# Fused transformer blocks, the first projection: x and the first weight unit lead the transfers, and x is turned between the unit's chunks

## Chip, cores and metric

The kernel runs on one core of one Trainium2 chip. The metric is the device time in microseconds (us) of one execution; lower is better.

## What is computed

Two stacked transformer blocks on x (256 tokens, 2048 channels, float32). The change touches only the first step of the first layer: a norm, and the product with the weights of queries, keys and values.

```python
def rms_norm(x, gain):
    xf = x.astype(jnp.float32)
    y = xf * lax.rsqrt(jnp.mean(xf * xf, axis=-1, keepdims=True) + EPS) * gain.astype(jnp.float32)
    return y.astype(x.dtype)

def first_block(x, ...):
    h = x
    for i in range(DEPTH):
        hn = rms_norm(h, mix_norm[i])
        # i == 0: mixer_a begins with qkv = h @ w_qkv, (256, 2048) x (2048, 3072)
        h = h + mixer_a(hn, ...)   # i == 1: mixer_b
        h = h + conv_ffn(rms_norm(h, ffn_norm[i]), ...)
    return rms_norm(h, final_norm)
# after it two layers of a second block (four attention kinds each), on the result
```

## The kernel before

All weights stream through in units of 1 MB (128 partitions x 2048 values). SyncE loads a unit into one of five `raw` buffers (`load_unit`, L216), ScalarE makes its rounded high part (`split_high`, L234) and VectorE the low rest, in place of `raw` (`split_low`, L242). TensorE multiplies each 128-row chunk with three products, high by high, low by high and high by low (`three`, L259 to L261), so that the result is near float32. Work on a unit is ordered by counting semaphores: `w_high`, `w_low`, and `w_used`, which TensorE raises after a unit. Since `high` has three buffers, the split of unit u waits until unit u-3 is used.

`qkv_product` (L773) is the first stage: 24 units, 6 column groups of 512 columns with 4 units each. Each unit holds 4 of the 16 row chunks; for each of the two 128-token tiles a unit takes 4 chunks x 3 matmuls, so 24 matmuls of 128x512 in all. The left operand, x transposed and multiplied by the norm's gain, in a high and a low part (`hh`, `hl`), is made once at the start, in four groups g of 512 channels. `Boundary` holds its steps:

- `turn(pe, g)` (L425 to L440): 8 transposes (L438) of the group into two banks, given by `SUM_BANK` = (4, 6, 0, 2).
- `high(act, g)` (L447): four ScalarE copies of 256 columns (L451) from the banks into `hh`, times the gain.
- `low(dve, g)` (L457): four VectorE steps (L462) into `hl`; the last raises `h_low`.
- `square(act, g)` (L480): sums of squares for the norm, which is applied only to the results.

The gains come from four tables (`mix_norm`, `ffn_norm`, `pre_norm_g_2`, `final_norm`), loaded as 112 rows, transposed once on TensorE (L918), copied by VectorE into `gain` (L882, semaphore `g_taken`).

The order is written out by hand for each engine. SyncE issues `ident` and the four tables (L816 to L820), then x group 0, unit 0, x group 1, unit 1, x groups 2 and 3, units 2 to 4. TensorE waits for the tables, transposes them, then turns x groups 0 to 3, one behind the other, and only then takes unit 0. ScalarE does `high(0)`, the split of unit 0, `high(1)`, the split of unit 1, `high(2)`, `high(3)`, then the split of unit 2; VectorE follows in the same order with the low parts. Everything behind this stage (attention, output product, feed-forward, the other layers) is not touched.

Of the kernel before, what the change touches and what calls it, by code (L numbers as in the profile page):

```python
# [21 lines left out]
F32 = mybir.dt.float32  # L22
F32R = mybir.dt.float32r
ALU = mybir.AluOpType
# [313 lines left out]


SUM_BANK = (4, 6, 0, 2)  # L340


class Boundary:
# [19 lines left out]
        return (0 if self.kind == "load" else 8, 16 if self.kind == "final" else 8, 2 if self.kind == "final" else 1)  # L363

    def bank(self, g, t):
        return self.c.bank[SUM_BANK[g] + t]

    def cols(self, t, g):
        return self.c.x[:, t, g * 512:(g + 1) * 512]
# [73 lines left out]

        return sum(b.kind in ("post", "end") for b in self.c.boundaries[0:self.n])

    def high(self, act, g):
        c = self.c  # L447
        act.wait_ge(c.x_turned, 4 * self.n + g + 1)
        for k in range(4):
            kt = 4 * g + k  # L450
            ins = act.activation(c.hh[:, kt, :], self.bank(g, k // 2)[:, k % 2 * S:(k % 2 + 1) * S], ACT.Copy,  # L451
                                 scale=c.gain[:, self.gain_col + kt:self.gain_col + kt + 1])
            if k % 2:
                ins.then_inc(c.h_high, 1)

    def low(self, dve, g):
        c = self.c  # L457
        for k in range(4):
            kt = 4 * g + k
            if k % 2 == 0:  # L460
                dve.wait_ge(c.h_high, 8 * self.n + 2 * g + k // 2 + 1)
            ins = dve.scalar_tensor_tensor(out=c.hl[:, kt, :], in0=self.bank(g, k // 2)[:, k % 2 * S:(k % 2 + 1) * S],  # L462
                                           scalar=c.gain[:, self.gain_col + kt:self.gain_col + kt + 1],
                                           in1=c.hh[:, kt, :].bitcast(F32), op0=ALU.mult, op1=ALU.subtract)
        ins.then_inc(c.h_low, 1)

    def square(self, act, g):

# [304 lines left out]
def qkv_product(c, consts, n_groups, per_group, take, loads, make_side):  # L773
# [12 lines left out]
    with st:  # L786
# [2 lines left out]
        taken = sem("taken")  # L789
        side = make_side(sb, sem, taken, bound)  # L790
        own, turned, cleared = (sem(x) for x in ("own", "turned", "cleared"))
        jobs = [(g, job) for g in range(n_groups) for job in side.jobs.get(g, ())]
        first_late = n_groups - (1 if side.lag < per_group else 2)
        assert all(len(side.jobs.get(g, ())) <= 4 for g in range(first_late))
# [3 lines left out]
        def group_before(j):  # L798

            g, rest = divmod(j - side.lag, per_group)  # L800
            return g - 1 if rest == 0 else -1
# [7 lines left out]
        @block.sync  # L809
        def _(sp):  # L810
            x = c.w["x"][0].rearrange("(t p) d -> p t d", p=P)

            def load_group(g):
                sp.dma_start(c.x[:, :, g * 512:(g + 1) * 512], x[:, :, g * 512:(g + 1) * 512]).then_inc(c.x_loaded[g], 16)

            sp.dma_start(c.ident[:, :], consts["ident"]).then_inc(g_loaded, 16)  # L816
            for name, at in (("mix_norm", GAIN_MIX), ("ffn_norm", GAIN_FFN), ("pre_norm_g_2", GAIN_PRE)):
                sp.dma_start(gain_rows[at:at + 2 * KT, :],
                             c.w[name].rearrange("l (k p) -> (l k) p", p=P)).then_inc(g_loaded, 16)
            sp.dma_start(gain_rows[GAIN_END:GAIN_END + KT, :],  # L820
                         c.w["final_norm"].rearrange("(k p) -> k p", p=P)).then_inc(g_loaded, 16)
            load_group(0)
            load_unit(c, sp, 0)
            load_group(1)
            load_unit(c, sp, 1)
            load_group(2)
            load_group(3)
            for u in range(2, RAW):
                load_unit(c, sp, u)
            preload(c, sp, loads)  # L830
            for j in range(n):
                load_unit(c, sp, u0 + j + RAW)

        @block.scalar
        def _(act):
            def side_work(g):
                if g in side.scalar:
                    side.scalar[g](act)

            def take_jobs(group):  # L840
                for i, (g, job) in enumerate(jobs):
                    if g == group:
                        act.wait_ge(turned, i + 1)
                        take_job(act, job, c.bank[i % 4]).then_inc(cleared, 1)

            act.wait_ge(g_taken, 1)
            bound.high(act, 0)
            split_high(c, act, u0)
            bound.high(act, 1)
            split_high(c, act, u0 + 1)  # L850
            bound.high(act, 2)
            bound.high(act, 3)
            for j in range(n):
                if j < n - 1:
                    split_high(c, act, u0 + j + AHEAD)
                if j < 2:
                    bound.square(act, 2 * j)
                    bound.square(act, 2 * j + 1)
                if j == 2:
                    bound.root(act)  # L860
                if j % per_group == 0:
                    side_work(j // per_group - 1)
                take_jobs(group_before(j))
            side_work(n_groups - 1)
            for g in range(first_late, n_groups):
                take_jobs(g)

        @block.vector
        def _(dve):
            chain = Chain(dve, own)  # L870

            def side_work(g, i):

                if g in side.vector and 0 <= i < len(side.vector[g]):
                    if i == 0:
                        dve.wait_ge(taken, 2 * (g + 1))
                    side.vector[g][i](chain)
                left[g] = chain.n

            dve.memset(c.eps[:, :], EPS)  # L880
            dve.wait_ge(g_turned, 1)
            dve.tensor_copy(c.gain[:, :], c.bank[2][:, 0:7 * KT]).then_inc(g_taken, 1)  # L882
            dve.wait_ge(g_taken, 1)
            first = c.gain[:, GAIN_PRE:GAIN_PRE + KT]
            dve.tensor_tensor(first, first, c.gain[:, GAIN_END:GAIN_END + KT], ALU.mult)
            bound.low(dve, 0)
            split_low(c, dve, u0)
            bound.low(dve, 1)
            split_low(c, dve, u0 + 1)
            bound.low(dve, 2)  # L890
            bound.low(dve, 3)
            for j in range(n):
                if j < n - 1:
                    split_low(c, dve, u0 + j + AHEAD)
                if j == 2:
                    bound.stats(dve)
                    side.before(chain)
                side_work(j // per_group - 1, j % per_group - side.wait)
                if j % per_group == per_group - 1:
                    take_group(dve, j // per_group)  # L900
            for i in range(len(side.vector.get(n_groups - 1, ()))):
                side_work(n_groups - 1, i)
            left[n_groups - 1] = chain.n

        @block.tensor
        def _(pe):
            def transposes(group):
                for i, (g, job) in enumerate(jobs):
                    if g == group:
                        pe.wait_ge(taken, 2 * (g + 1))  # L910
                        if left[g]:
                            pe.wait_ge(own, left[g])
                        if i >= 4:
                            pe.wait_ge(cleared, i - 3)
                        transpose_job(c, pe, job, c.bank[i % 4]).then_inc(turned, 1)

            pe.wait_ge(g_loaded, 80)
            pe.transpose(c.bank[2][:, 0:7 * KT], gain_rows[:, :], c.ident[0:7 * KT, 0:7 * KT]).then_inc(g_turned, 1)  # L918
            for g in range(3):
                bound.turn(pe, g)  # L920
            pe.wait_ge(g_taken, 1)
            bound.turn(pe, 3)
            for g in range(n_groups):
                if g >= 2:
                    pe.wait_ge(taken, 2 * (g - 1))
                for q in range(per_group):
                    u = u0 + g * per_group + q
                    transposes(group_before(g * per_group + q))
                    pe.wait_ge(c.w_low, u + 1)
                    if g == 0:  # L930
                        bound.await_chunks(pe, 4 * q)
                    wh, wl = split_view(c, u)
                    for t in range(TB):
                        out = c.bank[4 + 2 * (g % 2) + t][:, :]
                        for k in range(4):
                            kt = 4 * q + k
                            ins = three(pe, out, c.hh[:, kt, t * P:(t + 1) * P], c.hl[:, kt, t * P:(t + 1) * P],
                                        wh[:, k, :], wl[:, k, :], kt == 0, kt == KT - 1)
                    ins.then_inc(c.w_used, 1)
            for g in range(first_late, n_groups):  # L940
                transposes(g)
# [2099 lines left out]
```

## Time and profile before

| | |
|---|---|
| runs shown | 3349.14, 3349.6, 3351.03 us; median 3349.6 us |
| the profiled execution's own time | 3350.5 us |
| its span, first to last instruction | 3348.7 us |
| mean granted TensorE clock | 0.995 |
| busy: TensorE matmul, VectorE, ScalarE | 3290.2, 2020.5, 1630.5 us |
| what the transfers read from memory | 606.39 MB, 185 GB/s over the span |

A row of the timeline starts with the start and the duration in us, counted from the span's start. The engines are PE (TensorE matmul), PEld (TensorE weight load), DVE (VectorE), ACT (ScalarE) and SPq (SyncE's issue of a transfer). Behind a row, in brackets, stands how long the engine had been idle and what released it. Matmuls overlap in the pipeline, so the distance of two starts counts, not the duration of one. PEclk is the granted share of TensorE's full clock of 2.4 GHz; at 0.50 it is 1.2 GHz.

### The profile page before, as it was taken

How to read it: one execution, taken by the hardware profiler on the slowest of the kernel's cores; microseconds unless marked ns; L12 is line 12 of the kernel's file. 1: busy time of each engine (PE TensorE's matmuls, PEld its weight loads, DVE VectorE, ACT ScalarE, POOL GpSimd, SP SyncE). 2: the span in 40 equal slices, each digit the busy share in tenths (PEclk: the TensorE clock that was granted, in tenths of full speed). 3: DMA queues.
4: the chain of work that ended last, by engine and by line, in shares of the span. 5: the costliest groups of instructions: out<-in, count | busy, mean ns of one | idle time of the engine just before them, and what ended most of it. 6: DMA issues, size and time to landing. Idle time of an engine off the chain costs nothing. (4 is left out here: it accounts for less than half of the span.)

```text
span 3348.7 us, 43197 instructions
## 1 busy us (share of the span) xinstructions
PE 3290.2 (98%) x18176; PEld 2855.8 (85%) x18176; DVE 2020.5 (60%) x2448; ACT 1630.5 (49%) x1875; POOL 0.2 (0%) x4
## 2 busy tenths in 40 slices
PE   8999999999999999999999999999999999999998
PEld 7768888888888999998888888888898987898986
DVE  6765774774665555555666576576565654664654
ACT  5554553553444444443554355354454753464743
POOL 0000000000000000000000000000000000000000
PEclk9999999999999999999999999999999999999999
DMA  6525556556556555555555555555754446754544
GB/s 224 179 79 187 189 195 208 190 192 221 189 201 195 182 183 180 185 179 180 183 189 194 198 189 189 194 188 183 227 174 142 154 155 229 224 170 138 164 155 176
DMA packets 498937, 615.54 MB, mean 184 GB/s; under 512 B 21733, under 2 KB 383359, under 8 KB 497720
## 3 DMA queue, kind: packets, MB, share of 16 engines
q1 hardware_dynamic: 495288, 606.49, 54.7%
q10 hardware_dynamic: 3456, 6.29, 0.6%
q8 instruction: 144, 2.36, 0.3%
q14 instruction: 49, 0.40, 0.1%
HBM read 606.39 MB, written 12.63 MB: 185 GB/s over the span
## 5 line engine op out<-in xcount | busy, mean ns | idle before, releaser
L242 DVE TENSOR_TENSOR low<-raw,high 128x2048 fp32r<-128x2048 f32 (+3 forms) x564 | 1243.3, 2205 | 900.2 <-ACT high L234 895.5
L234 ACT ACTIVATE high<-raw 128x2048 fp32r<-128x2048 f32 (+3 forms) x564 | 1042.4, 1849 | 1259.2 <-PE bank L280 612.0
L270 PE MATMUL bank<-h,high 128*128 128x512 f32 x4672 | 1124.4, 393 | 3.0 <-PEq L1656 1.0
L270 PEld LDWEIGHTS bank<-h,high 128*128 128x128 f32 x4672 | 859.9, 188 | 178.1 <-issue 9.2
L280 PEld LDWEIGHTS bank<-h,low 128*128 128x128 f32 x4672 | 599.0, 191 | 22.7
L280 PE MATMUL bank<-h,low 128*128 128x256 f32 x4672 | 606.0, 283 | 0.0
L259 PE MATMUL bank<-high,y_high 128*128 128x512 f32 x1208 | 473.6, 392 | 4.0 <-DVE hy_tmp L2686 2.3
L261 PE MATMUL bank<-high,y_low 128*128 128x512 f32 x1208 | 471.5, 390 | 0.0
L260 PE MATMUL bank<-low,y_high 128*128 128x512 f32 x1208 | 471.4, 390 | 0.0
L259 PE MATMUL bank<-high,h 128*128 128x256 f32 (+4 forms) x1112 | 362.0, 326 | 1.9 <-PEq L1032 1.0
L261 PE MATMUL bank<-high,h 128*128 128x256 f32 (+4 forms) x1112 | 354.1, 318 | 0.0
L260 PE MATMUL bank<-low,h 128*128 128x256 f32 (+4 forms) x1112 | 353.8, 318 | 0.0
L259 PEld LDWEIGHTS bank<-high,y_high 128*128 128x128 f32 x1208 | 227.7, 188 | 51.4 <-DVE hy_tmp L2686 2.8
L261 PEld LDWEIGHTS bank<-high,y_low 128*128 128x128 f32 x1208 | 227.5, 188 | 47.8
L260 PEld LDWEIGHTS bank<-low,y_high 128*128 128x128 f32 x1208 | 227.7, 188 | 46.3
L259 PEld LDWEIGHTS bank<-high,h 128*128 128x128 f32 x1112 | 212.9, 191 | 16.8 <-issue 1.8
L260 PEld LDWEIGHTS bank<-low,h 128*128 128x128 f32 x1112 | 212.9, 191 | 13.6
L261 PEld LDWEIGHTS bank<-high,h 128*128 128x128 f32 x1112 | 212.4, 191 | 14.1
L1161 DVE SCALAR_TENSOR_TENSOR st_cv<-st_v,conv,st_cv 128x255 f32<-128x255 f32 x352 | 142.7, 480 | 0.0
L1087 ACT ACTIVATE st_cv<-st_v,conv 128x256 f32<-128x256 f32 x176 | 91.2, 591 | 4.9 <-DVE st_v L1151 4.9
L2517 ACT ACTIVATE hy_tmp<-bank 128x512 f32<-128x512 f32 x34 | 20.3, 598 | 114.7 <-PE bank L280 114.7
L2686 DVE TENSOR_TENSOR hy_tmp<-bank,hy_tmp 128x512 f32<-128x512 f32 x34 | 23.5, 692 | 80.9 <-ACT hy_tmp L2517 80.9
(263 smaller groups left out, 1884.5 us busy)
## 6 DMA issues: line engine op xcount, KB each, us to landing
raw<-in_w_up SPq DMA_DIRECT2D x176, 1024.0 KB, 5.0
raw<-in_w_down SPq DMA_DIRECT2D x88, 1024.0 KB, 5.1
raw<-in_w_in SPq DMA_DIRECT2D x84, 1024.0 KB, 5.0
raw<-in_b_w_qkv SPq DMA_DIRECT2D x72, 1024.0 KB, 4.9
raw<-in_w_out SPq DMA_DIRECT2D x32, 1024.0 KB, 5.0
raw<-in_a_w_qkv SPq DMA_DIRECT2D x24, 1024.0 KB, 5.0
raw<-in_b_w_o SPq DMA_DIRECT2D x24, 1024.0 KB, 5.0
raw<-in_a_w_o SPq DMA_DIRECT2D x16, 1024.0 KB, 5.0
```

The source lines that it names most:

```text
L234: act.activation(c.high[u % SPLIT][:, 0:n], c.raw[u % RAW][:, 0:n], ACT.Copy).then_inc(c.w_high, 1)
L242: dve.tensor_tensor(c.low[u % RAW][:, 0:n], c.raw[u % RAW][:, 0:n], c.high[u % SPLIT][:, 0:n].bitcast(F32), ALU.subtract).then_inc(c.w_low, 1)
L259: pe.matmul(out, lh, rh, start=start, stop=False, skip_group_check=skip)
L260: pe.matmul(out, lh, rl, start=False, stop=False, skip_group_check=skip)
L261: return pe.matmul(out, ll, rh, start=False, stop=stop, skip_group_check=skip)
L270: pe.matmul(banks[:, i, :], wh[:, k, i * P:(i + 1) * P], c.h[:, k0 + k, :, :].rearrange("p a n -> p (a n)"), start=k0 + k == 0, stop=False ...
L280: ins = pe.matmul(banks[:, i, 0:S], wl[:, k, i * P:(i + 1) * P], c.hh[:, k0 + k, :], start=False, stop=k0 + k == KT - 1, skip_group_check= ...
L1087: act.activation(cv[:, par, q, :], v[:, par, q, :], ACT.Identity, bias=taps[:, 3, ch:ch + 1], scale=taps[:, 1, ch:ch + 1]).then_inc(centre ...
L1161: ins = dve.scalar_tensor_tensor(out=out, in0=v[:, par, q, src], scalar=taps[:, tap, ch:ch + 1], in1=out, op0=ALU.mult, op1=ALU.add)
L2517: act.activation(self.tmp[:, n % 2, :, :], c.psum[:, bank:bank + 2, S:2 * S], ACT.Copy).then_inc(self.halved, 1)
L2686: dve.tensor_tensor(tmp, c.psum[:, bank:bank + 2, 0:S], tmp, ALU.add).then_inc(self.taken, 2)
```

## The change

1. SyncE issues x group 0 first, then unit 0 as two transfers of two chunks each (semaphores `first_in` and `arrived[0]`), and then x group 1, unit 1, x groups 2 and 3 and the other units as before.
2. ScalarE issues `ident` and the four tables, and behind them runs one activation of a single column on `eps`, which brings the load of its function table (ACT_TABLE_LOAD) to this place.
3. Unit 0 is split in halves of 1024 columns. ScalarE: the first two steps of `high(0)`, first half, the other two steps, second half; VectorE likewise.
4. TensorE turns x group 0 only, and takes unit 0 chunk by chunk: chunk 0 after the first half (`first_low`), then x group 1 is turned, chunk 1, chunk 2, x group 2 is turned, chunk 3. Units 1 to 3 follow as before, but x group 3 is turned ahead of unit 2.
5. The banks of the first boundary become `LOAD_BANK` = (0, 2, 6, 0) in place of (4, 6, 0, 2); the sums of column group 0 are in banks 4 and 5, as before. `turn(pe, 3)` waits for `h_low` of group 0 (`await_chunks(pe, 0)`), whose banks it takes over.

```diff
 SUM_BANK = (4, 6, 0, 2)
+LOAD_BANK = (0, 2, 6, 0)
...
-    def high(self, act, g):
+    def high(self, act, g, pair=None):
...
-        for k in range(4):
+        for k in range(4) if pair is None else (2 * pair, 2 * pair + 1):
...
-        ins.then_inc(c.h_low, 1)
+        if pair != 0:
+            ins.then_inc(c.h_low, 1)
...
-            sp.dma_start(c.ident[:, :], consts["ident"]).then_inc(g_loaded, 16)
...
             load_group(0)
-            load_unit(c, sp, 0)
+            for i in range(2):
+                sp.dma_start(first_raw[:, 2 * i:2 * i + 2, :], c.units[0][:, 2 * i:2 * i + 2, :]).then_inc(
+                    c.arrived[0] if i else first_in, 16)
             load_group(1)
...
+            act.dma_start(c.ident[:, :], consts["ident"]).then_inc(g_loaded, 16)
...
+            act.wait_ge(eps_set, 1)
+            act.activation(c.stat[:, 5, 0:1], c.eps[:, 0:1], ACT.Copy)
             act.wait_ge(g_taken, 1)
-            bound.high(act, 0)
-            split_high(c, act, u0)
+            for i in range(2):
+                bound.high(act, 0, i)
+                act.wait_ge(c.arrived[0] if i else first_in, 16)
+                act.activation(c.high[0][:, i * 1024:(i + 1) * 1024], c.raw[0][:, i * 1024:(i + 1) * 1024],
+                               ACT.Copy).then_inc(c.w_high if i else first_high, 1)
             bound.high(act, 1)
             split_high(c, act, u0 + 1)
             bound.high(act, 2)
...
-            for g in range(3):
-                bound.turn(pe, g)
+            bound.turn(pe, 0)
             pe.wait_ge(g_taken, 1)
-            bound.turn(pe, 3)
+            wh, wl = split_view(c, u0)
+            for k in range(4):
+                if k % 2 == 0:
+                    pe.wait_ge(c.w_low if k else first_low, 1)
+                else:
+                    bound.turn(pe, 1 + k // 2)
+                for t in range(TB):
+                    ins = three(pe, c.bank[4 + t][:, :], c.hh[:, k, t * P:(t + 1) * P], c.hl[:, k, t * P:(t + 1) * P],
+                                wh[:, k, :], wl[:, k, :], k == 0, False)
+            ins.then_inc(c.w_used, 1)
             for g in range(n_groups):
...
-                for q in range(per_group):
+                for q in range(1 if g == 0 else 0, per_group):
                     u = u0 + g * per_group + q
+                    if g == 0 and q == 2:
+                        bound.await_chunks(pe, 0)
+                        bound.turn(pe, 3)
                     transposes(group_before(g * per_group + q))
```

**TensorE, from the program's start to its first matmuls of unit 0** (L438 and L439 are the transposes of x; `low_49` is unit 0's low part). Before:

```order
L918 MATMUL bank<-ident,st_gain_rows 128x112 [waits st1_gains_loaded]
L438 MATMUL bank<-ident,x 128x128 [waits x_loaded0]
L438 MATMUL bank<-ident,x 128x128 x7
L438 MATMUL bank<-ident,x 128x128 [waits x_loaded1]
L438 MATMUL bank<-ident,x 128x128 x7
L438 MATMUL bank<-ident,x 128x128 [waits x_loaded2]
L438 MATMUL bank<-ident,x 128x128 x7
L438 MATMUL bank<-ident,x 128x128 [waits x_loaded3,st1_gains_taken]
L438 MATMUL bank<-ident,x 128x128 x7
L259 MATMUL bank<-high,h 128x512 [waits h_low,w_low]
```

Now:

```order
L933 MATMUL bank<-ident,st_gain_rows 128x112 [waits st1_gains_loaded]
L439 MATMUL bank<-ident,x 128x128 [waits x_loaded0]
L439 MATMUL bank<-ident,x 128x128 x7
L259 MATMUL bank<-high,h 128x512 [waits st1_first_low,st1_gains_taken]
L260 MATMUL bank<-low_49,h 128x512
L261 MATMUL bank<-high,h 128x512
L259 MATMUL bank<-high,h 128x512
L260 MATMUL bank<-low_49,h 128x512
L261 MATMUL bank<-high,h 128x512
L439 MATMUL bank<-ident,x 128x128 [waits x_loaded1]
L439 MATMUL bank<-ident,x 128x128 x7
```

Six matmuls of unit 0 moved ahead of the turning of groups 1 to 3.

**TensorE, where unit 1 ends and unit 2 begins**, in the changed kernel (`low_50` is unit 1, `low_51` unit 2):

```order
L260 MATMUL bank<-low_50,h 128x512
L261 MATMUL bank<-high,h 128x512
L439 MATMUL bank<-ident,x 128x128 [waits x_loaded3,h_low]
L439 MATMUL bank<-ident,x 128x128 x7
L259 MATMUL bank<-high,h 128x512 [waits h_low,w_low]
L260 MATMUL bank<-low_51,h 128x512
```

The turning of group 3 stood ahead of unit 0 and stands now behind the last matmul of unit 1.

**ScalarE, from the split of unit 1 to that of unit 2**, in the changed kernel (L452 is `high`, L234 the split of a unit):

```order
L234 ACTIVATE high<-raw 128x2048 [waits w_arrived1]
L452 ACTIVATE h<-bank,gain 128x256 [waits x_turned]
L452 ACTIVATE h<-bank,gain 128x256 x3
L452 ACTIVATE h<-bank,gain 128x256 [waits x_turned]
L452 ACTIVATE h<-bank,gain 128x256 x3
L234 ACTIVATE high<-raw 128x2048 [waits w_arrived2]
L482 ACTIVATE y,sum_squares<-x 128x512 [waits h_low]
```

Nothing moved here: `high(3)` stands ahead of the split of unit 2, as it did before.

## Rows read from the trace of the kernel before

**Rows 1.** The page's busy times (us, share of span, instructions)

```profile
PE 3290.2 (98%) x18176; PEld 2855.8 (85%) x18176; DVE 2020.5 (60%) x2448; ACT 1630.5 (49%) x1875; POOL 0.2 (0%) x4
```

**Rows 2.** What TensorE waited for, 0 to 160 us (in total, times, longest)

```profile
PE bank L438 <- DMA x<-in_x: 7.2, 3, 3.1
PE bank L918 <- DMA st_gain_rows<-in_final_norm: 4.2, 1, 4.2
```

**Rows 3.** Timeline of SyncE's transfer issues (start us, duration us, line, tile<-source)

```profile
0.73 0.40 SPq L816 DMA_DIRECT2D ident<-const_ident  x1
...
2.58 0.42 SPq L820 DMA_DIRECT2D st_gain_rows<-in_final_norm  x1
3.04 0.42 SPq L814 DMA_DIRECT2D x<-in_x  x1
3.51 0.46 SPq L224 DMA_DIRECT2D raw<-in_a_w_qkv  x1
```

**Rows 4.** Timeline of TensorE, 0 to 30 us

```profile
7.70 1.97 PE L438 MATMUL bank<-ident,x 128*128 128x128 f32 x8 [3.07 <-DMA x<-in_x]
11.73 1.97 PE L438 MATMUL bank<-ident,x 128*128 128x128 f32 x8 [2.06 <-DMA x<-in_x]
15.79 3.67 PE L438 MATMUL bank<-ident,x 128*128 128x128 f32 x16 [2.10 <-DMA x<-in_x]
19.12 0.78 PE L259 MATMUL bank<-high,h 128*128 128x512 f32 x1
...
20.96 0.39 PE L260 MATMUL bank<-low,h 128*128 128x512 f32 x1
21.19 0.39 PE L261 MATMUL bank<-high,h 128*128 128x512 f32 x1
```

**Rows 5.** Timeline of ScalarE, 0 to 90 us

```profile
9.75 1.28 ACT L451 ACT_TABLE_LOAD   x1 [9.75 <-PE bank L438]
11.05 1.57 ACT L451 ACTIVATE h<-bank,gain 128x256 fp32r<-128x256 f32 x4
12.49 1.93 ACT L234 ACTIVATE high<-raw 128x2048 fp32r<-128x2048 f32 x1
...
25.78 1.92 ACT L234 ACTIVATE high<-raw 128x2048 fp32r<-128x2048 f32 x1 [0.46 <-PE bank L261]
...
31.22 1.92 ACT L234 ACTIVATE high<-raw 128x2048 fp32r<-128x2048 f32 x1 [1.07 <-PE bank L261]
```

**Rows 6.** Timeline of VectorE, 0 to 90 us

```profile
11.92 1.66 DVE L462 SCALAR_TENSOR_TENSOR h<-bank,gain,h 128x256 fp32r<-128x256 f32 x4 [6.78 <-ACT h L451]
14.45 2.29 DVE L242 TENSOR_TENSOR low<-raw,high 128x2048 fp32r<-128x2048 f32 x1 [0.87 <-ACT high L234]
```

**Rows 7.** Transfer issues of the whole kernel (count, KB each, median us to landing)

```profile
bias_skewed_rows<-bias_rows ACTq DMA_DIRECT2D x24, 256.0 KB, 6.0
...
b_bias<-bias_skewed_rows SPq DMA_DIRECT2D x32, 64.0 KB, 3.8
...
st_gain_rows<-in_final_norm SPq DMA_DIRECT2D x1, 8.0 KB, 1.6
```

**Rows 8.** Timeline of TensorE, 2334 to 2352 us

```profile
2335.59 0.39 PE L261 MATMUL bank<-high,y_low 128*128 128x512 f32 x1
2340.34 1.97 PE L438 MATMUL bank<-ident,x 128*128 128x128 f32 x8 [4.36 <-DVE x L384]
...
2344.67 0.63 PE L259 MATMUL bank<-high,y_high 128*128 128x512 f32 x1
2345.10 0.55 PE L260 MATMUL bank<-low,y_high 128*128 128x512 f32 x1
```

**Rows 9.** The same place in stretches (length, busy times, PEclk, DMA share, GB/s)

```profile
2336.00:2340.00 4.00, 0.00 (x0) 0.00 (x0) 3.20 (x3) 0.76 (x1) 0.00 (x0) 0.82 0.74 243
2340.00:2345.00 5.00, 4.66 (x15) 4.08 (x16) 1.49 (x3) 2.65 (x8) 0.00 (x0) 0.50 0.04 16
```

**Rows 10.** Timeline of TensorE, 2842 to 2862 us

```profile
2860.68 1.03 PE L438 MATMUL bank<-ident,x 128*128 128x128 f32 x8
```

More of the change, by code:

```diff
@@ L365, in bank @@
     def bank(self, g, t):
-        return self.c.bank[SUM_BANK[g] + t]
+        return self.c.bank[(LOAD_BANK if self.kind == "load" else SUM_BANK)[g] + t]
     def cols(self, t, g):
@@ L454, in high, with low @@
                 ins.then_inc(c.h_high, 1)
-    def low(self, dve, g):
+    def low(self, dve, g, pair=None):
         c = self.c
-        for k in range(4):
+        for k in range(4) if pair is None else (2 * pair, 2 * pair + 1):
             kt = 4 * g + k
@@ L791, in qkv_product @@
         own, turned, cleared = (sem(x) for x in ("own", "turned", "cleared"))
+        first_in, first_high, first_low, eps_set = (sem(x) for x in ("first_in", "first_high", "first_low", "eps_set"))
+        first_raw = c.raw[0][:, :].rearrange("p (k n) -> p k n", k=4)
         jobs = [(g, job) for g in range(n_groups) for job in side.jobs.get(g, ())]
@@ L814, in load_group @@
                 sp.dma_start(c.x[:, :, g * 512:(g + 1) * 512], x[:, :, g * 512:(g + 1) * 512]).then_inc(c.x_loaded[g], 16)
-            sp.dma_start(c.ident[:, :], consts["ident"]).then_inc(g_loaded, 16)
[L817 to L821, printed above, removed]
             load_group(0)
-            load_unit(c, sp, 0)
+            for i in range(2):
+                sp.dma_start(first_raw[:, 2 * i:2 * i + 2, :], c.units[0][:, 2 * i:2 * i + 2, :]).then_inc(
+                    c.arrived[0] if i else first_in, 16)
             load_group(1)
@@ L844, in take_jobs @@
                         take_job(act, job, c.bank[i % 4]).then_inc(cleared, 1)
-            act.wait_ge(g_taken, 1)
-            bound.high(act, 0)
-            split_high(c, act, u0)
+            act.dma_start(c.ident[:, :], consts["ident"]).then_inc(g_loaded, 16)
+            for name, at in (("mix_norm", GAIN_MIX), ("ffn_norm", GAIN_FFN), ("pre_norm_g_2", GAIN_PRE)):
+                act.dma_start(gain_rows[at:at + 2 * KT, :],
+                              c.w[name].rearrange("l (k p) -> (l k) p", p=P)).then_inc(g_loaded, 16)
+            act.dma_start(gain_rows[GAIN_END:GAIN_END + KT, :],
+                          c.w["final_norm"].rearrange("(k p) -> k p", p=P)).then_inc(g_loaded, 16)
+            act.wait_ge(eps_set, 1)
+            act.activation(c.stat[:, 5, 0:1], c.eps[:, 0:1], ACT.Copy)
+            act.wait_ge(g_taken, 1)
+            for i in range(2):
[3 more added lines that the diff above has]
+                               ACT.Copy).then_inc(c.w_high if i else first_high, 1)
             bound.high(act, 1)
@@ L878, in side_work @@
                 left[g] = chain.n
-            dve.memset(c.eps[:, :], EPS)
+            dve.memset(c.eps[:, :], EPS).then_inc(eps_set, 1)
             dve.wait_ge(g_turned, 1)
@@ L885, in _ @@
             dve.tensor_tensor(first, first, c.gain[:, GAIN_END:GAIN_END + KT], ALU.mult)
-            bound.low(dve, 0)
-            split_low(c, dve, u0)
+            for i in range(2):
+                bound.low(dve, 0, i)
+                dve.wait_ge(c.w_high if i else first_high, 1)
+                at = slice(i * 1024, (i + 1) * 1024)
+                dve.tensor_tensor(c.low[0][:, at], c.raw[0][:, at], c.high[0][:, at].bitcast(F32),
+                                  ALU.subtract).then_inc(c.w_low if i else first_low, 1)
             bound.low(dve, 1)
```

## The prediction

> **What bounds the kernel now.** I read the page's busy times first: TensorE is busy 98% of the span [rows 1], so whatever moves TensorE's stream moves the end. Next I read TensorE's waits in the first stage, 0 to 160 us: 7.2 us for x and 4.2 us for the tables [rows 2], both at the very start. Between those and the end of the stage it waits for nothing. Then the timelines of the first 30 us, engine by engine. SyncE spends 0.73 to 3.04 us on `ident` and the tables before it issues x group 0 [rows 3]; that group is turned from 7.70, the others from 11.73 and 15.79, and unit 0 starts at 19.12 [rows 4]. From there on TensorE runs without a gap, one unit in 31.22 - 25.78 = 5.44 us: ScalarE's splits there are released by TensorE's end of units 0 and 1 [rows 5]. So unit 2 starts at about 31.0. That number is the one to beat: all later units run at TensorE's pace, so what unit 2 gains or loses is the gain or loss of the kernel. A measurement of this kernel can tell about 0.2% from no change, 6.7 us; the whole start-up of 19.1 us is 0.6%.
>
> **Part 1, transfers.** Five issues leave SyncE ahead of x; x group 0 is issued at 0.73 instead of 3.04, 2.31 us earlier [rows 3]. Its time to landing stays (it had 3.04 to 7.70, 4.66 us), so it lands at 5.39. The halves of unit 0 cost one more issue, 0.47 us, beside the transfers themselves: nothing, since group 1 is wanted late. Everything behind moves up as far; group 3, last of the x groups, was turned by 19.46 at the latest without a wait inside its row [rows 4], so all of x and unit 1, which is ahead of it in the queue, are there by 17.2 now, and their users come later, except unit 1 (wanted at 16.9). Group 2 was already there at 15.79, 13.5 now, and unit 1 is ahead of that too, so I count no wait.
>
> **Part 2, the tables.** ScalarE issues them from 0.73 on at the same step, the last at 2.58. Alone they landed in 1.6 us [rows 7], at 4.2, ahead of x; now they share the transfer engines with x. Bounds: 1.6 us from below (a gain isn't possible, since x is what is waited for), and 6.0 from above, ScalarE's own 256 KB transfers beside the weight stream; 64 KB beside it took 3.8 [rows 7]. The last table has 8 KB, so I take 2.5: at 5.1, with the transposition of the tables turning starts at 5.6. Each us later is a us more: at 3.8 it is 1.3 us more, at 6.0 3.5 us more. The Trainium skill (DMA: Bandwidth & Descriptors, "Issuing engines are not separate DMA queues") says that transfers from several engines interleave on the same 16 and that only issue time is saved, and its latency table gives up to 2 us for a memory access under high load. By it the tables would land at about 2.58 + 1.6 + 1.8 = 6.0, an estimate from that page, and the sum would be 0.9 us worse, 5.55; no row before shows small tables beside x.
>
> **Part 3, up to chunk 0.** Turning takes 1.97, to 7.6. ScalarE's function table load (1.28) stood between turning and `high(0)` [rows 5] and is now over long before. ScalarE: two steps of `high` 0.72, half a split. From 0.36 a step at 256 columns and 1.80 from one split's start to the next start at 2048, 1024 columns take 0.98. So pair 0 from 7.65 to 8.4, half 0 to 9.45, pair 1 to 10.1, half 1 to 11.1. VectorE: 0.41 a step of `low`, 2.29 a whole split, so about 1.2 half a one [rows 6]: low half 0 is done at 10.7, low half 1 at 12.6. Unit 0 starts at **10.75 instead of 19.12**, 8.4 us earlier. If this were all, it would be a gain of 8.4.
>
> **Part 4, units 0 and 1.** After a pause TensorE runs at half speed: starts of 128x512 matmuls are 0.43 apart (2344.67 to 2345.10) in the stretch with a granted clock of 0.50, that is 1.2 GHz [rows 8, 9], and 0.23 at full [rows 4]. In the new start it had paused from 7.6 to 10.75. Chunk 0: 6 x 0.43 = 2.6, to 13.35. Turning group 1 at half speed 1.97, to 15.35. Chunk 1, partly fast, 1.5; chunk 2, 1.4; turning group 2 at full speed about 0.9 (1.03 with its tail [rows 10]); chunk 3, 1.4: unit 0 ends at 20.2. Unit 1 needs group 1: ScalarE's `high(1)` 15.4 to 16.85, split of unit 1 to 18.75, VectorE's low part 2.29, 21.05. Unit 1 runs from **21.1 to 26.55** instead of 25.5 to 31.0. So far 4.4 us are gained.
>
> **Part 5, group 3 behind unit 1.** Here a wait is added. TensorE turns group 3 at 26.55 to 27.6. ScalarE's next work in its order is `high(3)`, and the split of unit 2 is queued behind that, though unit 2's data has long been there. So a chain stands between units 1 and 2 that was hidden before: turning 1.05, `high(3)` 1.45, split of unit 2 1.93, low part 2.29, with the handovers 6.8 us. Unit 2 starts at **33.35 instead of 31.0: 2.35 us later** than before.
>
> **Part 6, the clock.** TensorE pauses from 27.6 to 33.35, 5.75 us. The nearest row is the pause of 4.36 us at 2336: the granted clock fell in it (mean 0.82) and was 0.50 in the 5 us behind it [rows 9]; the transposes took 1.97 and matmuls stayed slow until 2345.10 [rows 8], 4.8 us from the resumption at 2340.34. Unit 2 then has 4.9 / 0.43 = about 11.5 slow starts, each 0.20 longer: **2.3 us**. Bounds: nothing if the clock holds (against all rows with such a pause), 2.6 if it takes as long as the 5.2 us from 15.79 to 20.96 at the start [rows 4].
>
> **Part 7, behind.** Unit 3's split on ScalarE comes after four squares and is ready at about 37.6, unit 2 ends at 41.1; the norm's statistics and units 4 and 5 are ready 5 us or so ahead of TensorE. No further wait, and nothing wins the time back, since TensorE is the bound.
>
> **The sum**: 2.35 + 2.3 = 4.65 us slower. Against the profiled execution's own time of 3350.5 it is 3355.2; that execution lies 0.9 above the median of the runs shown, so against the median 3349.6 + 4.65 = 3354.3. That is 0.14%, less than the measurement can tell.
>
> **The rivals.**
> A. *The tables come late.* ScalarE's small transfers are queued beside the stream of x and weights, TensorE waits for all five before it turns anything, and every later start up to unit 2 shifts one to one. At 6.0 us to landing it is 3.5 more, 3349.6 + 4.65 + 3.5 = 3357.8. It passes the 6.7 us from a landing at about 7.2 us on (4.6 us after the issue). For it: the median of ScalarE's transfers [rows 7]. Against it: those were 256 KB, with writes to memory; these are 8 to 64 KB. This makes the kernel slower by over 0.2%.
> B. *The clock holds over the pause.* Then 2.3 falls away: 3352.0. All rows speak against it.
> C. *The gain arrives*: the split of unit 2 is not held by group 3, and units run on from 26.55: 31.0 - 26.55 = 4.4 us less, and 0.9 more spent on turning: 3346.1. ScalarE's order speaks against it. It would need the engine to run out of its order. Even this stays inside 0.2%: a gain of over 6.7 would need nearly all of the 8.4 of part 3.
>
> **How the numbers follow.** My forecast 0.77, A 0.14, B 0.05, C 0.04. The start may be 0.7 earlier than I take it (tables at once, shorter landing) or 1 later; the clock costs 1.3 to 2.6; so the forecast's own range is 3352.5 to 3356. The range takes in A up to its price and B's neighbourhood: 3351.3 to 3357.8. Only A passes 0.2%, and about two thirds of it; with a little for unnamed waits slower has 0.12, faster 0.02, same 0.86.
>
> **What would show it.** In the new profile: x group 0 turned from about 5.6; the first matmul of unit 0 near 10.75; unit 1 near 21.1; a TensorE wait of 5 to 6 us before unit 2, released by VectorE's low part, and matmuls 0.43 apart behind it; unit 2's first matmul near 33.35. A first turning at 7.5 or later would show rival A; a stretch at 0.23 right behind the wait, B; no wait, C. A wait at a later unit, or a clock that stays low past unit 2, would make the forecast wrong.

## The result, and the profile after

| | us | against before |
|---|---|---|
| before, 11 runs | 3349.6 (3348.02 to 3351.03) | |
| changed, 11 runs | 3358.03 (3355.9 to 3361.31) | ratio 1.0027, interval 1.0018 to 1.0035 |
| forecast | 3354.3, range 3351.3 to 3357.8 | |

The kernel is 8.4 us slower, 0.25%, where 4.65 was forecast; the median lies just above the range. The profiled execution took 3359.23 us, its span is 3357.0, against 3350.5 and 3348.7 before, so it shows 8.3 us more of span.

The page's busy times of the changed kernel stand beside [rows 1]: TensorE works as long as before and the span is longer.

```profile
PE 3292.1 (98%) x18176; PEld 2857.2 (85%) x18176; DVE 2020.1 (60%) x2449; ACT 1628.4 (49%) x1877; POOL 0.2 (0%) x4
```

TensorE's waits in the first stage, 0 to 160 us, answer to [rows 2] (in total, times, longest). Before there were 11.4 us of them, now 17.8:

```profile
PE bank L933 <- DMA st_gain_rows<-in_final_norm: 8.3, 1, 8.3
PE bank L259 <- DVE low L242: 6.2, 2, 5.8
PE bank L259 <- DVE low L901: 3.3, 1, 3.3
```

The timeline of TensorE, 0 to 50 us, answers to [rows 4]:

```profile
8.28 0.45 PE L933 MATMUL bank<-ident,st_gain_rows 112*128 112x112 f32 x1 [8.28 <-DMA st_gain_rows<-in_final_norm]
8.52 1.91 PE L439 MATMUL bank<-ident,x 128*128 128x128 f32 x8
13.73 0.76 PE L259 MATMUL bank<-high,h 128*128 128x512 f32 x1 [3.29 <-DVE low L901]
...
24.12 0.50 PE L259 MATMUL bank<-high,h 128*128 128x512 f32 x1 [0.37 <-DVE low L242]
...
29.70 1.03 PE L439 MATMUL bank<-ident,x 128*128 128x128 f32 x8
36.52 0.79 PE L259 MATMUL bank<-high,h 128*128 128x512 f32 x1 [5.78 <-DVE low L242]
37.11 0.63 PE L260 MATMUL bank<-low,h 128*128 128x512 f32 x1
...
39.24 0.54 PE L259 MATMUL bank<-high,h 128*128 128x512 f32 x1
39.62 0.40 PE L260 MATMUL bank<-low,h 128*128 128x512 f32 x1
```

The reader is to see four things. Group 0 is turned at 8.52, not at 5.6, because the tables' transposition at 8.28 waits for the last table. x group 0 itself had landed at 5.34, where 5.39 was forecast, and then stood waiting for the tables for 3 us. From there to unit 1 all follows as forecast: 5.2 us to chunk 0 (forecast 5.15), and unit 1 at 24.12. Group 3 is turned at 29.70, and then there is the wait of 5.78 us, released by VectorE's low part (forecast 5.75). Then unit 2's matmuls start 0.43 apart up to 39.24. Before, unit 2 began at 31.0 and unit 3 at 36.4; now they begin at 36.52 and 43.52.

Who makes the wait is on ScalarE (answers to [rows 5]) and VectorE (to [rows 6]):

```profile
0.73 0.45 ACTq L846 DMA_DIRECT2D ident<-const_ident  x1
...
2.77 0.61 ACTq L850 DMA_DIRECT2D st_gain_rows<-in_final_norm  x1
...
22.40 1.57 ACT L452 ACTIVATE h<-bank,gain 128x256 fp32r<-128x256 f32 x4 [0.66 <-PE bank L439]
30.77 1.57 ACT L452 ACTIVATE h<-bank,gain 128x256 fp32r<-128x256 f32 x4 [6.80 <-PE bank L439]
32.21 1.93 ACT L234 ACTIVATE high<-raw 128x2048 fp32r<-128x2048 f32 x1
```

```profile
34.17 2.29 DVE L242 TENSOR_TENSOR low<-raw,high 128x2048 fp32r<-128x2048 f32 x1 [0.87 <-ACT high L234]
```

`high(3)` follows the turning at 30.77, the split of unit 2 is queued behind it at 32.21, the low part runs 34.17 to 36.46. ScalarE had been idle for 6.80 us ahead of `high(3)`, from 23.97 on, and unit 2's data had landed at 17.96.

The tables' landing, from the transfers of 0 to 40 us (count, KB, us from issue to landing), answers to [rows 7]:

```profile
ident<-const_ident ACTq DMA_DIRECT2D x1, 64.0 KB, 4.2
...
st_gain_rows<-in_mix_norm ACTq DMA_DIRECT2D x1, 16.0 KB, 4.8
...
st_gain_rows<-in_final_norm ACTq DMA_DIRECT2D x1, 8.0 KB, 5.5
```

The last one took 5.5 us, where it had taken 1.6 ahead of x. From 5 to 8 us the transfer engines moved 385 GB/s with a DMA share of 1.04, so the tables' last microseconds fell into a full stream.

**The rest of the 8.3 us.** I laid TensorE's instructions of the two executions side by side, the n-th beside the n-th. At the end of unit 2 the changed kernel is 7.1 us late, and stays so through all other 21 units. Then the distance changes mainly at three places: by -1.6 at the start of the output product (209 to 212 us before), by +1.4 near 2404 and by +1.7 near 2856 us; a smaller step of -0.3 lies near 2345. All are stretches behind a pause of TensorE that both kernels have (1.7, 2.9 and 7.1 us long at the three places). The stretches of before, in the columns of [rows 9]:

```profile
209.00:213.00 4.00, 4.00 (x13) 3.16 (x12) 2.76 (x2) 3.01 (x2) 0.00 (x0) 0.62 0.00 0
...
2405.00:2410.00 5.00, 5.00 (x45) 5.00 (x44) 1.25 (x1) 1.08 (x1) 0.00 (x0) 1.00 1.06 305
...
2855.00:2860.00 5.00, 4.91 (x22) 4.06 (x23) 5.00 (x10) 2.57 (x4) 0.00 (x0) 1.00 0.01 2
```

and the same places in the changed kernel:

```profile
216.00:220.00 4.00, 4.00 (x19) 3.28 (x18) 2.65 (x2) 3.12 (x2) 0.00 (x0) 1.00 0.02 4
...
2410.00:2415.00 5.00, 5.00 (x38) 5.00 (x36) 1.25 (x1) 1.08 (x1) 0.00 (x0) 0.82 1.04 300
...
2860.00:2865.00 5.00, 4.08 (x12) 3.00 (x11) 5.00 (x11) 4.04 (x7) 0.00 (x0) 0.50 0.01 2
```

PEclk tells it: at the first place only the kernel before runs at half clock for some microseconds (0.62), at the other two only the changed one is still slow (0.82 and 0.50 against 1.00). So in this pair of profiles 7.1 us come from the start, and 1.2 from how long the half clock happened to last at places that the change doesn't touch.

### The profile page after: what moved, and what is told of

The parts are those of the page before. It is cut to its first block and busy times, and to the rows that moved or that the text cites. A ratio compares the mean times of both kernels' runs of the same rounds, so it can differ in the third digit from the quotient of the medians.

```text
span 3357.0 us, 43205 instructions
## 1 busy us (share of the span) xinstructions
PE 3292.1 (98%) x18176; PEld 2857.2 (85%) x18176; DVE 2020.1 (60%) x2449; ACT 1628.4 (49%) x1877; POOL 0.2 (0%) x4
## 5 line engine op out<-in xcount | busy, mean ns | idle before, releaser
L234 ACT ACTIVATE high<-raw 128x2048 fp32r<-128x2048 f32 (+3 forms) x563 | 1039.0, 1846 | 1254.9 <-PE bank L280 612.4
L259 PE MATMUL bank<-high,h 128*128 128x256 f32 (+4 forms) x1112 | 365.1, 328 | 11.4 <-DVE low L242 6.2
L452 ACT ACTIVATE h<-bank,gain 128x256 fp32r<-128x256 f32 x96 | 37.7, 474 | 84.0 <-PE bank L439 83.9
```

Of the source, the lines that this page charges most:

```text
L234: act.activation(c.high[u % SPLIT][:, 0:n], c.raw[u % RAW][:, 0:n], ACT.Copy).then_inc(c.w_high, 1)
L259: pe.matmul(out, lh, rh, start=start, stop=False, skip_group_check=skip)
```

## The experiments

Three theories were left. T1: the wait ahead of unit 2 is ScalarE's queueing, and behind it a slow clock. T2: the tables are late because they share the transfer engines with x (against: a transfer issued by ScalarE is slow in itself). T3: giving x the lead is worth its 2.3 us where nothing hangs on the tables. Each kernel but the tables alone has 11 runs; before had 27 runs beside the first four (median 3349.74) and 33 beside the others (3350.07). The ratios are estimated from all runs and aren't quotients of the medians. An interval that contains 1 means that the kernel can't be told from before.

| kernel | median us | ratio to before, interval |
|---|---|---|
| changed | 3358.03 | 1.0027, 1.0018 to 1.0035 |
| group 3 turned early | 3349.35 | 1.0001, 0.9992 to 1.001 |
| wait filled | 3354.39 | 1.0015, 1.0006 to 1.0024 |
| unit 2's split first | 3351.57 | 1.0008, 0.9999 to 1.0017 |
| tables alone (one run) | 3362.39 | |
| tables lead | 3355.82 | 1.0021, 1.0012 to 1.003 |
| tables on both queues, group 3 early | 3346.98 | 0.9993, 0.9984 to 1.0002 |
| only the loads of the change | 3348.04 | 0.9995, 0.9986 to 1.0004 |
| both queues, group 3 early, unit 2's split first | 3345.52 | 0.9988, 0.998 to 0.9997 |

### Group 3 turned right behind unit 0

```diff
             ins.then_inc(c.w_used, 1)
+            bound.await_chunks(pe, 0)
+            bound.turn(pe, 3)
...
-                    if g == 0 and q == 2:
-                        bound.await_chunks(pe, 0)
-                        bound.turn(pe, 3)
```

> The changed kernel with one edit: x group 3 is turned right behind unit 0 instead of behind unit 1. Theory (the wait ahead of unit 2 is the chain turning of group 3, high(3), split, low part, and TensorE's slow stretch behind it): the wait of 5.8 us disappears, ScalarE's high(3) and the split of unit 2 run beside unit 1, unit 2 starts at about 30 to 31 instead of 36.5 and at full clock, so 7 to 8 us less than the changed kernel, 3349 to 3351. Rival (unit 2 waits for its data or for another engine): the wait stays, less than 2 us gained.

Measured: 3349.35, 8.7 us less than the changed kernel. TensorE's timeline:

```profile
23.80 1.04 PE L439 MATMUL bank<-ident,x 128*128 128x128 f32 x8
24.59 0.47 PE L259 MATMUL bank<-high,h 128*128 128x512 f32 x1
...
30.63 0.50 PE L259 MATMUL bank<-high,h 128*128 128x512 f32 x1 [0.31 <-DVE low L242]
```

Group 3 is turned at 23.80, unit 1 follows at once, and unit 2 starts at 30.63 after 0.31 us of waiting, at full clock (0.50 is the length of a first matmul at full clock). That is 0.3 ahead of the kernel before, although the tables were late here too (8.24). So T1 holds: with group 3 turned earlier the loss is gone. The kernel can't be told from before then; it isn't shown to be faster.

### The wait filled with other matmuls

```diff
                         bound.turn(pe, 3)
+                        for _ in range(23):
+                            pe.matmul(c.bank[3][:, :], c.hh[:, 0, 0:P], c.h[:, 0, :, :].rearrange("p a n -> p (a n)"),
+                                      start=True, stop=True, skip_group_check=True)
```

The 23 products are added work; nothing reads them.

> The changed kernel with 23 more matmuls of 128x512 into a free bank, in the wait between the turning of group 3 and unit 2; nothing reads them. Theory (the clock falls in the wait): unit 2 starts at the same place, near 36.5, but at 0.23 us a matmul from the first on; 1.4 us less than the changed kernel in the same execution (7 slow starts of 0.20), up to 2.3. Rival (the slow starts come from what unit 2's matmuls read, not from the pause): the first 7 stay at 0.43 and nothing is gained.

Measured: 3354.39, 3.6 us less than the changed kernel, though it does more work. TensorE's timeline:

```profile
30.04 1.04 PE L439 MATMUL bank<-ident,x 128*128 128x128 f32 x8
30.83 5.50 PE L955 MATMUL bank<-h 128*128 128x512 f32 x23
36.87 0.50 PE L259 MATMUL bank<-high,h 128*128 128x512 f32 x1 [0.53 <-DVE low L242]
```

Unit 2 starts at 36.87, where it started without them (0.35 later, and the tables were 0.3 later too), and its 24 starts are 0.23 apart behind the first, which takes 0.33; the first lasts 0.50 us, where it lasted 0.79. So the slow starts come from the pause, not from unit 2. The direct price of the slow stretch in the changed kernel's profile is 36.52 to 39.62 for seven starts, 3.1 us instead of 1.6: 1.5 us. Two runs further down show 2.5 (the tables lead) and 2.7 (the tables alone). Side by side the filled kernel's profile is 1.1 us ahead of the changed one from unit 3 on and 2.7 at the end; the other 1.6 arise in the later stretches at half clock. What makes the 3.6 between the medians can't be read from one profile of each.

### Unit 2's split ahead of `high(3)` and `low(3)`

```diff
             bound.high(act, 2)
+            split_high(c, act, u0 + 2)
             bound.high(act, 3)
             for j in range(n):
-                if j < n - 1:
+                if 0 < j < n - 1:
                     split_high(c, act, u0 + j + AHEAD)
```

(and likewise `split_low` on VectorE; group 3 is still turned behind unit 1.)

> The changed kernel with the split of unit 2 put ahead of high(3) on ScalarE and ahead of low(3) on VectorE; group 3 is still turned behind unit 1. Theory (queueing in ScalarE's order makes the wait): only high(3) and low(3) stay in the chain, the wait falls from 5.8 to about 2.6 us, 3.2 us less, and up to 1.4 more if the clock doesn't fall in so short a pause. Rival (the wait is the turning and x group 3 itself): no more than 1 us gained.

Measured: 3351.57, 6.5 us less than the changed kernel. The wait did not shrink to 2.6 us ahead of unit 2, as I expected. It vanished there and came back one unit later:

```profile
29.22 1.04 PE L439 MATMUL bank<-ident,x 128*128 128x128 f32 x8
30.01 0.47 PE L259 MATMUL bank<-high,h 128*128 128x512 f32 x1
...
38.48 0.50 PE L259 MATMUL bank<-high,h 128*128 128x512 f32 x1 [2.75 <-DVE low L242]
```

Unit 2 starts at 30.01 right behind the turning, since it multiplies the chunks of group 2. Group 3 belongs to unit 3. What unit 3 waits for, 2.75 us at 38.48, is its split, which on ScalarE stands behind `high(3)` and four squares:

```profile
22.95 1.93 ACT L234 ACTIVATE high<-raw 128x2048 fp32r<-128x2048 f32 x1
30.29 1.57 ACT L452 ACTIVATE h<-bank,gain 128x256 fp32r<-128x256 f32 x4 [5.42 <-PE bank L439]
...
34.19 1.92 ACT L234 ACTIVATE high<-raw 128x2048 fp32r<-128x2048 f32 x1
```

The clock didn't fall in this pause: unit 3's matmuls run at full pace. So queueing alone made the wait ahead of unit 2, which is T1 in its sharper form: the split of unit 2 had no need of group 3.

### The tables alone

```diff
+            sp.wait_ge(g_loaded, 80)
             load_group(0)
```

> The changed kernel, but SyncE's first transfer waits until ScalarE's five table transfers have landed. Only the landing time is read. Theory (the tables are late because they share the transfer engines with x and unit 0): the last table lands 1.6 to 1.9 us after its issue, at about 4.6, and TensorE transposes it then. Rival (a transfer issued by ScalarE takes longer in itself): again about 5.5 us, at 8.3. The whole kernel is then some microseconds later than the changed one, since x starts late.

Measured, TensorE's timeline:

```profile
4.45 0.45 PE L934 MATMUL bank<-ident,st_gain_rows 112*128 112x112 f32 x1 [4.45 <-DMA st_gain_rows<-in_final_norm]
8.89 1.97 PE L439 MATMUL bank<-ident,x 128*128 128x128 f32 x8 [3.99 <-DMA x<-in_x]
```

Issued by ScalarE with nothing beside them, the tables are there at 4.45, 1.9 us after the last issue at 2.58. It is the company of x and unit 0, not ScalarE's queue: T2 holds as far as that. That what they share is the transfer engines fits the full stream of 5 to 8 us, but no run separates it from other things they might share. Behind it x group 0 lands and is turned at 8.89, and the rest repeats the changed kernel, a wait of 5.8 us included.

### The tables ahead of x

The table transfers are issued by SyncE ahead of x, as before the change; all else is the changed kernel.

> The changed kernel with ident and the four tables issued by SyncE ahead of x, as before the change; ScalarE issues nothing. Theory (tables beside x land late, and the start shifts one to one): tables land at about 4.2, x group 0 at 7.7, group 0 is turned at 7.7 instead of 8.5, all later starts up to unit 2 move up by 0.8 us, and the wait of 5.8 us ahead of unit 2 stays: 0.8 less than the changed kernel, about 3357. Rival (giving x the lead is worth its 2.3 us): slower than the changed kernel.

Measured: 3355.82, 2.2 us less than the changed kernel, where 0.8 was expected. TensorE's timeline:

```profile
4.29 0.45 PE L933 MATMUL bank<-ident,st_gain_rows 112*128 112x112 f32 x1 [4.29 <-DMA st_gain_rows<-in_final_norm]
7.54 1.97 PE L439 MATMUL bank<-ident,x 128*128 128x128 f32 x8 [2.80 <-DMA x<-in_x]
...
35.50 0.80 PE L259 MATMUL bank<-high,h 128*128 128x512 f32 x1 [5.78 <-DVE low L242]
...
40.78 0.48 PE L259 MATMUL bank<-high,h 128*128 128x512 f32 x1
...
43.63 0.39 PE L259 MATMUL bank<-high,h 128*128 128x512 f32 x1
```

Turning starts at 7.54 and unit 2 at 35.50, both 1.0 us earlier than in the changed kernel. The slow stretch cost 2.5 us here (35.50 to 40.78 for twelve starts), 1.0 more than in the changed kernel's profile, so that unit 3 starts at 43.63 against 43.52. In this pair of profiles the first stage thus gains nothing in sum; the spans differ by the 2.2 us that arise in later stretches. What is shown is the 1.0 us up to unit 2: giving x the lead with all five tables beside it costs 1.0 us there and gains nothing.

### Tables on both queues, ahead of x, and group 3 early

```diff
+            sp.dma_start(c.ident[:, :], consts["ident"]).then_inc(g_loaded, 16)
+            sp.dma_start(gain_rows[GAIN_MIX:GAIN_MIX + 2 * KT, :],
+                         c.w["mix_norm"].rearrange("l (k p) -> (l k) p", p=P)).then_inc(g_loaded, 16)
             load_group(0)
...
-            for name, at in (("mix_norm", GAIN_MIX), ("ffn_norm", GAIN_FFN), ("pre_norm_g_2", GAIN_PRE)):
+            for name, at in (("ffn_norm", GAIN_FFN), ("pre_norm_g_2", GAIN_PRE)):
                 act.dma_start(gain_rows[at:at + 2 * KT, :],
```

> Group 3 turned right behind unit 0, and the tables issued ahead of x from both engines: ident and mix_norm by SyncE, the other three by ScalarE, so that x is issued at 1.66. Theory: tables land by 3.5, x group 0 at 6.3, unit 0 starts at 11.5 and unit 2 at 28.4 instead of 30.6 with the tables late: 2.2 less than with group 3 turned early alone, about 3347. Rival (tables split over two engines land late too): turning starts at 8 or later and nothing is gained on that kernel.

Measured: 3346.98, 2.4 less than with group 3 early alone. TensorE's timeline:

```profile
4.99 0.45 PE L935 MATMUL bank<-ident,st_gain_rows 112*128 112x112 f32 x1 [4.99 <-DMA st_gain_rows<-in_final_norm]
6.03 1.97 PE L439 MATMUL bank<-ident,x 128*128 128x128 f32 x8 [0.60 <-DMA x<-in_x]
11.29 0.77 PE L259 MATMUL bank<-high,h 128*128 128x512 f32 x1 [3.29 <-DVE low L903]
...
27.12 0.50 PE L259 MATMUL bank<-high,h 128*128 128x512 f32 x1 [0.17 <-DVE low L242]
```

The last table is there at 4.99: issued at 1.65, it took 3.3 us, with x issued at 1.66 beside it; the other four took 1.8 to 2.1. That still hides behind x, which is turned at 6.03. All is 2.4 to 3.5 us earlier than in the kernel with late tables (13.68 and 30.63 there, 11.29 and 27.12 here); 2.4 come from the tables, the rest from a slow stretch that ended sooner, at 15.18 instead of 19.36. Against before the interval still contains 1.

### Only the loads of the change

The kernel before, with `ident` and the tables issued by ScalarE and x first on SyncE. Unit 0 is whole, and all four groups are turned ahead of it.

> The kernel before with one part of the change: ScalarE issues ident and the tables, SyncE begins with x; unit 0 whole, all four groups turned ahead of it. Theory (the old order is bound by the landing of x group 3, and late tables have time): turning starts at 8.5, later than before, but group 3 is there 2.3 us earlier and unit 0 starts at about 16.9 instead of 19.1; no wait comes up, 2.2 us less than before, about 3347.5. Rival (late tables cost here too): no change against before, or slower.

Measured: 3348.04, 2.0 less than before, within what can be told apart. TensorE's timeline:

```profile
8.49 0.45 PE L918 MATMUL bank<-ident,st_gain_rows 112*128 112x112 f32 x1 [8.49 <-DMA st_gain_rows<-in_final_norm]
8.73 3.62 PE L438 MATMUL bank<-ident,x 128*128 128x128 f32 x16
13.97 3.68 PE L438 MATMUL bank<-ident,x 128*128 128x128 f32 x16 [1.62 <-DMA x<-in_x]
17.77 0.50 PE L259 MATMUL bank<-high,h 128*128 128x512 f32 x1
18.11 0.39 PE L260 MATMUL bank<-low,h 128*128 128x512 f32 x1
...
23.35 0.39 PE L259 MATMUL bank<-high,h 128*128 128x512 f32 x1
```

The tables are late (8.49), but the old order has time for that: the next wait is for x group 2 at 13.97, 1.8 us earlier than before, and unit 0 starts at 17.77 instead of 19.12. Expected was 16.9; x lands 0.5 us later than moved up rigidly, and turning groups 2 and 3 takes its 3.7 us at half clock. (At the start of the program PEclk reads 1.00 even there; the half clock shows in the durations, 3.7 us for 16 transposes where 8 take 1.03 at full clock.) But unit 0 runs at full clock from its first matmul on, while before it had four slow starts, to 20.96. So unit 1 starts at 23.35 instead of 25.52, 2.2 us earlier: 1.35 from the transfers, and 0.8 because the slow stretch was over sooner, which nobody had planned. T3 holds in this profile; the medians, 2.0 us apart, don't prove it.

### All three together

> As the kernel with the tables on both queues and group 3 turned behind unit 0, and also the split of unit 2 ahead of high(3) and low(3). Theory (unit 2 needs only group 2 and its split; group 3 is needed by unit 3): the last wait of about 0.3 us ahead of unit 2 goes, at most 0.5 us less than that kernel, 3346.5 to 3347.5, within its scatter. Rival (unit 3's split is now late): a wait ahead of unit 3.

Measured: 3345.52, ratio to before 0.9988, interval 0.998 to 0.9997: 4.5 us less than before and 12.5 less than the change. In its first stage TensorE waits for nothing but these and, for 0.6 us, x group 0:

```profile
PE bank L937 <- DMA st_gain_rows<-in_final_norm: 5.0, 1, 5.0
PE bank L259 <- DVE low L904: 3.3, 1, 3.3
```

No wait is left ahead of unit 2 or 3. Against the kernel without the last edit the difference of 1.5 us is within the scatter. This version beats both kernels.

## Why the prediction was wrong

The mechanism and the sign were right, the size was not. Part 1 held for x group 0, which landed at 5.34 (5.39). The other steps:

- **Part 2, the tables: the step that failed.** I took 2.5 us from issue to landing; the last table took 5.5 (issued at 2.77, not 2.58, since the issues took 0.45 to 0.61 us each instead of 0.40 to 0.42). Turning began at 8.52 instead of 5.6: 2.9 us. This was rival A, at nearly its price, which I gave 0.14. The nearest row was ScalarE's own transfers with 6.0 us [rows 7]; I went by the size of the table instead. The rule of the Trainium skill (DMA: Bandwidth & Descriptors, "Issuing engines are not separate DMA queues") is that all queues run on the same 16 engines. The runs agree with it, since ScalarE's last table landed within 1.9 us of its issue when nothing ran beside it; they don't show the engines as the cause. The landing near 6.0 that I had estimated from that page's latency table was still 2.3 us short of the measured 8.28.
- **Parts 3 and 4** held: turning to chunk 0 5.2 us (5.15), turning to unit 1 15.6 us (15.5). One sum in them was off without moving anything: the terms of unit 0 add up to 20.55, not 20.2, and unit 1 waited for its own split either way.
- **Part 5** held in place and size: 5.78 us, released by the low part. Its sentence that the split is queued behind `high(3)` was right. The experiment with the split moved shows what I had not said: unit 2 does not need group 3 at all.
- **Part 6** held in kind, with 1.5 instead of 2.3 us in the profile; two other runs with the same pause show 2.5 and 2.7, so the upper bound of 2.6 was reached twice in three executions. By the part's own rule that bound would have been 2.4 (12 starts, each 0.20 longer).
- **Part 7** was right on the first stage and wrong behind it. I took all later stages as rigid. They shift by 1.4 to 1.7 us, either way, at places where TensorE pauses and the clock is slow for a varying time. In the profile this adds 1.2 us.

The sum with measured terms: unit 2 at 36.52 instead of 31.0, 5.5, and 1.5 for the slow starts make 7.0 (7.1 side by side); with 1.2 behind it 8.3. So two errors pulled against each other by luck: unit 2 was 3.2 us later than forecast and the slow stretch in this profile cost 0.8 less; with the 1.2 behind them that is the 3.6 by which 8.3 passes 4.65. With slow starts of 2.5 or 2.7 us, as in the two other runs, the first stage alone would make 8.1 to 8.3, an estimate; how the 8.4 between the medians divides among the parts is not known.

Rival B (the clock holds) is refuted by the slow starts and by the filled wait; rival C by the wait. The rival that came true had been written down, and the chain behind it shifts one to one, so its chance should have been the larger one.

## What to carry to other kernels

When a step is moved back in one engine's order, look at what is queued behind its consumers on the other engines: here eight transposes put behind a unit held up a split that had no need of them, so that unit 0 began 5.4 us earlier and unit 2 5.5 us later (late tables are 2.9 us of that). Small transfers that everything waits for go ahead of the bulk, not beside it; issuing them from two engines ahead of x gave the gain that issuing them beside x had lost (2.4 us at unit 0, with group 3 early in both). For a small transfer beside a full stream take the landing time of transfers beside a stream, whatever its size.

## What the runs showed of the hardware

- The five transfers of 8 to 64 KB, issued by ScalarE beside x and a weight unit, took 4.2 to 5.5 us to land in the changed kernel (4.1 to 5.9 in the other runs with this order); ahead of the stream 1.6 to 1.9.
- One such transfer, issued at the same moment as x group 0, took 3.3 us while those issued 0.5 to 0.9 us earlier took 1.8 to 2.1 (1.8 to 2.2 in a second kernel with this order).
- After the same pause of 5.8 us TensorE ran at half clock for 2.7 us of unit 2 in one execution, 5.3 in another and 5.7 in a third. A pause of 2.75 us left the clock up in the one execution that had it. Its length alone doesn't tell: in the kernel before, TensorE paused for 2.86 us up to 2400.55, and from 2400.1 to 2403.4 its granted clock was 0.50.
- The changed kernel's runs scatter over 5.4 us, those of before beside them over 3.0. The profiles show stretches at half clock that come and go in parts of the program that are the same; that this makes all of the scatter wasn't tested.
